# A closing norm whose last two feature tiles are squared one by one, and a feed-forward entry whose coarse products go first

## The reference, cut to what matters

```
def _rmsnorm(x, g):
    y = xf * lax.rsqrt(jnp.mean(xf * xf, axis=-1, keepdims=True) + EPS)
    return (y * g)
def _swiglu(x, w_up, w_down):
    g, u = jnp.split(x @ w_up, 2, axis=-1)
    return (jax.nn.silu(g) * u) @ w_down
for layer in range(DEPTH):
    x = x + 0.5 * _rmsnorm(_swiglu(_rmsnorm(x, ng[0]), w_ffn_up[layer, 0], w_ffn_down[layer, 0]), ng[1])
    h = _rmsnorm(x, ng[2])
    h = mixer(h)
    x = x + _rmsnorm(h, ng[3])
    x = x + 0.5 * _rmsnorm(_swiglu(_rmsnorm(x, ng[4]), w_ffn_up[layer, 1], w_ffn_down[layer, 1]), ng[5])
```

## Time and profile before

| | us |
|---|---|
| median of 3 runs | 2816.47 (2815.74 to 2819.28) |
| the profiled execution | 2812.93 |
| its span in the trace | 2811.2 |
| PE busy | 2674.3 (95%) |
| DVE busy | 1547.3 (55%) |
| ACT busy | 1154.2 (41%) |
| POOL busy | 273.4 (10%) |

### The profile page before, as it was taken

How to read it: one execution, slowest core, us unless ns; L and a number is a source line. 1 busy time by engine, 2 the same in 40 slices (tenths; PEclk the granted TensorE clock), 3 DMA queues, 4 the chain that set the end, 5 groups by cost and what they waited for, 6 DMA issues and landing times.

```text
span 2811.2 us, 51786 instructions
## 1 busy us (share of the span) xinstructions
PE 2674.3 (95%) x22016; PEld 2509.7 (89%) x22016; DVE 1547.3 (55%) x1978; ACT 1154.2 (41%) x1515; POOL 273.4 (10%) x294
## 2 busy tenths in 40 slices
PE   7998999899999899999999989999999989988998
PEld 7997887899999886699999978799999978877998
DVE  5546835655555445465465543465555558446554
ACT  4334444444433344343344333343343335435432
POOL 1000004100100225110010000010010000042000
PEclk9999999999999999999999999999999999998999
DMA  5544532454544535444455453455455444134543
GB/s 192 164 146 132 150 85 66 153 164 147 166 163 142 187 114 164 136 143 161 147 171 165 138 168 108 128 166 164 147 168 164 139 144 150 57 101 143 165 142 100
DMA packets 415626, 404.23 MB, mean 144 GB/s; under 512 B 14786, under 2 KB 411950, under 8 KB 415086
## 3 DMA queue, kind: packets, MB, share of 16 engines
q1 hardware_dynamic: 411348, 397.42, 44.9%
q0 software_dynamic: 4096, 4.20, 0.5%
HBM read 385.19 MB, written 16.39 MB: 143 GB/s over the span
## 4 chain that ended last, share of the span: by engine, by line
PE 88%; DVE 7%; ACT 2%; POOL 2%; issue 1%; DMA 0%; SPq 0%; DVEq 0%; POOLq 0%; ACTq 0%
PE psum L351 22%; PE psum L352 22%; PE psum L353 22%; POOL fbuf L406 1%; DVE x L537 1%; DVE y L535 1%; PE psum L2641 1%; PE psum L389 1%; PE psum L1115 1%; PE psum L1098 1%; PE psum L984 1%; DVE xn_lo L470 1%; PE psum L2040 1%; DVE w_lo L333 1%; PE psum L985 1%
## 5 line engine op out<-in xcount | busy, mean ns | idle before, releaser
L333 DVE TENSOR_TENSOR w_lo<-raw,w_hi 128x2048 fp32r<-128x2048 f32 (+3 forms) x366 | 753.4, 2058 | 555.5 <-ACT w_hi L326 555.4
L351 PE MATMUL psum<-xn_hi,w_hi 128*128 128x288 f32 x3296 | 987.2, 300 | 20.4 <-DVE xn_lo L1690 7.5
L352 PE MATMUL psum<-xn_lo,w_hi 128*128 128x288 f32 x3296 | 978.6, 297 | 0.0
L353 PE MATMUL psum<-xn_hi,w_lo 128*128 128x288 f32 x3296 | 975.2, 296 | 0.0
L326 ACT ACTIVATE w_hi<-raw 128x2048 fp32r<-128x2048 f32 (+3 forms) x366 | 623.9, 1705 | 785.2 <-PE psum L353 720.9
L351 PEld LDWEIGHTS psum<-xn_hi,w_hi 128*128 128x128 f32 x3296 | 623.9, 189 | 31.7 <-issue 16.4
L353 PEld LDWEIGHTS psum<-xn_hi,w_lo 128*128 128x128 f32 x3296 | 626.8, 190 | 0.0
L352 PEld LDWEIGHTS psum<-xn_lo,w_hi 128*128 128x128 f32 x3296 | 625.4, 190 | 0.4
L352 PE MATMUL psum<-h_lo,w_hi 128*128 128x288 f32 x1408 | 415.5, 295 | 0.0
L353 PE MATMUL psum<-h_hi,w_lo 128*128 128x288 f32 x1408 | 415.0, 295 | 0.0
L351 PE MATMUL psum<-h_hi,w_hi 128*128 128x288 f32 x1408 | 413.3, 294 | 0.0
(11 more groups left out here) (561 smaller groups left out, 3126.1 us busy)
## 6 DMA issues: line engine op xcount, KB each, us to landing
raw<-w_ffn_up SPq DMA_DIRECT2D x176, 1024.0 KB, 5.1
raw<-w_ffn_down SPq DMA_DIRECT2D x64, 768.0 KB, 4.4
raw<-w_ffn_down SPq DMA_DIRECT2D x64, 640.0 KB, 4.0
raw<-gdn_w_in SPq DMA_DIRECT2D x32, 1024.0 KB, 5.7
raw<-mlstm_w_in SPq DMA_DIRECT2D x12, 1024.0 KB, 5.4
raw<-gdn_w_out SPq DMA_DIRECT2D x8, 1024.0 KB, 6.8
raw<-cache_mla_latent SPq DMA_DIRECT2D x64, 128.0 KB, 2.2
a_split<-cache_mla_latent SPq DMA_DIRECT2D x64, 128.0 KB, 2.3
```

Source lines behind the costliest of these rows:

```text
L333: dve.tensor_tensor(wview(w_lo[slot(u, i)], u), wview(raw[u % NRAW], u), wview(w_hi[slot(u, i)], u).bitcast(F32), ALU.subtract).then_inc(l ...
L351: pe.matmul(out, wh[:, k, c], hi(k), start=st, stop=False)
L352: pe.matmul(out, wh[:, k, c], lo(k), start=False, stop=False)
L353: last = pe.matmul(out, wl[:, k, c], hi(k), start=False, stop=sp_)
```

## The change

Three edits. (1) In `act_square_y`, the last pair (i = 3) is squared tile by tile: tile 6 when PE has finished m = 0 of the last unit (a new semaphore `half_used`), tile 7 when the unit is done. Each raises `sq_ready`, so that a closing now counts five squares instead of four (`squares_before`). DVE takes tile 6 behind the first, tile 7 behind the second. (2) PE's product of `sq_total` moves from behind the last unit to between its m = 0 and its m = 1 (`pe_leave_part`); its waits move with it. The products of tiles 6 and 7 each wait for their own square. (3) In `pe_ffn` each tile k is done in two passes: first the 8 matmuls that need the coarse part of x alone (they wait for `xhi_ready`), then the 4 with its rest (they wait for `xlo_ready`).

```
-        def pe_unit(pe, u, outs, hi, lo, start, stop, i=0, ready=None, late=0):
+        def pe_unit(pe, u, outs, hi, lo, start, stop, i=0, ready=None, late=0, leave=None):
...
+                if leave is not None and m == 0:
+                    last.then_inc(half_used, 1)
+                    pe_leave_part(pe, leave)
...
+        half_used = sem("half_used")
+        squares_before = lambda q: H * q + q // 2
...
+        def pe_leave_part(pe, n):
+
+            pe.wait_ge(y_copied, H * n + 1)
+            pe.wait_ge(sq_sum, summed(2 * n + 1))
+            pe.matmul(psum[:, 1, 0:T], ones, sq_total, start=True, stop=False)
+
         def pe_leave_sums(pe, n):
 
-            q = 2 * n + 1
-            pe.wait_ge(y_copied, H * n + 1)
-            pe.wait_ge(sq_sum, summed(q))
-            pe.matmul(psum[:, 1, 0:T], ones, sq_total, start=True, stop=False)
-            pe.wait_ge(sq_ready, H * q + H)
             for k in range(2 * H - 2, 2 * H):
+                pe.wait_ge(sq_ready, squares_before(2 * n + 1) + k - H + 2)
                 last = pe.matmul(psum[:, 1, 0:T], ones, sq[:, k, :], start=False, stop=k == KC - 1)
...
-            dve.wait_ge(sq_ready, H * (2 * n + 1) + i + 1)
             for k in (2 * i, 2 * i + 1):
+                dve.wait_ge(sq_ready, squares_before(2 * n + 1) + i + 1 + (i == H - 1) * (k % 2))
                 last = dve.tensor_scalar(y[:, k, :], psum[:, k, 0:T], gain(l, g, k), None, ALU.mult)
...
+            if i == H - 1:
+                act.wait_ge(half_used, n + 1)
+                act.activation(sq[:, 2 * i, :], psum[:, 2 * i, 0:T], ACT.Square).then_inc(sq_ready, 1)
+                act.wait_ge(unit_used, u + 1)
+                act.activation(sq[:, 2 * i + 1, :], psum[:, 2 * i + 1, 0:T], ACT.Square).then_inc(sq_ready, 1)
+                return
...
             for k in range(KC):
-                pe.wait_ge(xlo_ready, entered(n) + k + 1)
+                pe.wait_ge(xhi_ready, entered(n) + k + 1)
                 for g, (hi, lo) in enumerate(first_two):
                     wh, wl = wview(hi, u0 + g), wview(lo, u0 + g)
                     for m in range(2):
                         out, c = psum[:, 4 + 2 * g + m, 0:T], slice(m * P, (m + 1) * P)
                         pe.matmul(out, wh[:, k, c], xn_hi[:, k, :], start=k == 0, stop=False)
-                        pe.matmul(out, wh[:, k, c], xn_lo[:, k, :], start=False, stop=False)
-                        last = pe.matmul(out, wl[:, k, c], xn_hi[:, k, :], start=False, stop=k == KC - 1)
+                        pe.matmul(out, wl[:, k, c], xn_hi[:, k, :], start=False, stop=False)
+                pe.wait_ge(xlo_ready, entered(n) + k + 1)
+                for g, (hi, lo) in enumerate(first_two):
+                    wh = wview(hi, u0 + g)
+                    for m in range(2):
+                        out, c = psum[:, 4 + 2 * g + m, 0:T], slice(m * P, (m + 1) * P)
+                        last = pe.matmul(out, wh[:, k, c], xn_lo[:, k, :], start=False, stop=k == KC - 1)
                     if k == KC - 1:
                         last.then_inc(unit_used, 1)
```

More of the change, by code:

```diff
@@ L382, in trunk @@
         entered = lambda n: sum(cuts(m) for m in range(n))
+        half_used = sem("half_used")
+        squares_before = lambda q: H * q + q // 2
         def pe_sum_squares(pe, q, i):
-            pe.wait_ge(sq_ready, H * q + i + 1)
+            pe.wait_ge(sq_ready, squares_before(q) + i + 1)
             for k in (2 * i, 2 * i + 1):
@@ L400, in pool_sums @@
             done, chunks = steps_before(q), range(2, H if q % 2 == 0 else H - 1)
-            pool.wait_ge(sq_ready, H * q + (2 if q % 2 else H))
+            pool.wait_ge(sq_ready, squares_before(q) + (2 if q % 2 else H))
             pool.tensor_tensor(sq_part, sq[:, 0:2, :], sq[:, 2:4, :], ALU.add).then_inc(sum_step, 1)
             for j, i in enumerate(chunks):
-                pool.wait_ge(sq_ready, H * q + i + 1)
+                pool.wait_ge(sq_ready, squares_before(q) + i + 1)
                 pool.wait_ge(sum_step, done + j + 1)
@@ L543, in pe_out @@
                 pe_unit(pe, u0 + i, [psum[:, 2 * i, 0:T], psum[:, 2 * i + 1, 0:T]], hi, lo, True, True,
-                        ready=ready if i == 0 else None)
+                        ready=ready if i == 0 else None, leave=n if i == H - 1 else None)
             pe_leave_sums(pe, n)
@@ L608, in pe_ffn @@
                     pe_unit(pe, u0 + 2 * PAIRS + DU * i + q, [psum[:, 2 * i, 0:T], psum[:, 2 * i + 1, 0:T]],
-                            lambda k: h_hi[:, k0 + k, :], lambda k: h_lo[:, k0 + k, :], q == 0, q == DU - 1)
+                            lambda k: h_hi[:, k0 + k, :], lambda k: h_lo[:, k0 + k, :], q == 0, q == DU - 1,
+                            leave=n if i == H - 1 and q == DU - 1 else None)
                     k0 += nk
```

## The result

The changed kernel takes 2831.09 us (median of 5, 2829.89 to 2833.60) against 2816.44 (median of 5, 2814.79 to 2819.28): ratio 1.0055, 95% interval 1.0044 to 1.0066. It is 14.65 us slower. The forecast was 2823.8 us, slower by 7.3, with a range up to 2831.0; the direction held, the size was half of what came, and the result lies 0.1 us beyond the range.

What follows compares the result with a forecast made beforehand. PE was taken to set the time except at boundaries between sublayers. Closings -2.4 us, low clock behind entries +8.5 and sums delayed by DVE +1.2 made +7.3, so 2823.8 us, range 2812 to 2831.

Steps and rivals of the forecast that it cites:

- The closing of a feed-forward: Closing behind the last unit: +0.49 us moved product, -0.24 shorter last square, -0.49 tile 6's product under cover; net -0.24.
- The entry: Feed-forward entry: PE starts 0.72 us earlier, but POOL's sum still releases the next work; no direct gain, longer second wait.
- The price of a low stretch: Behind the entry's wait for POOL, each stretch at granted clock 0.50 costs PE its whole 1.71 us.
- The displacement: Entry's end: DVE's split of the fourth unit gets in front of POOL's last step, making POOL's sum 2.3 us late.
- I take five of seven: Behind PE's wait for POOL at seven feed-forward entries, five get a stretch at granted clock 0.50: +8.5 us.
- an edge: PE waits: 2.37 us was followed by a low clock, 2.35 was not, so the limit was put near 2.4 us.
- I count half a case: Feed-forward entries: DVE getting ahead of POOL's last step, 2.3 us late each time, counted as half a case: +1.2 us.
- the closings together: All twelve closings, including PE's added wait in four mixers: -2.4 us, with ends at -4 and +0.5.
- a stand of 0.1 us for POOL's total: Mid unit in each of four mixers: PE waits 0.1 us for POOL's closing sum; +0.5 us in all.
- the forecast's own upper end: Top of the forecast's case: low clock behind all seven entries' waits and two sums delayed by DVE, 2830.7 us.
- the clock mostly holds: Rival: none to three of seven waits behind the entries bring a low clock; 2814.1 to 2819.2 us, chance 0.38.

Runs made afterwards that it cites:

- the closing edits alone: Kernel before plus split squares of tiles 6 and 7 and the moved `sq_total` product, feed-forward entry as before: 2815.30 us against 2815.43, ratio 0.9997.
- the entry edit alone: Kernel before plus only the feed-forward entry's coarse-part matmuls first, closings as before: 2824.93 us against 2815.43, ratio 1.0033.

## Why the prediction was right and wrong

Right, by its own steps:
- *The closing of a feed-forward.* -0.24 us each was forecast, and -0.24 to -0.25 is what the traces of the change and of the closing edits alone have. The root comes 1.59 us behind the last matmul's start; 1.58 was forecast.
- *The entry.* No direct gain, PE's first wait at 2.70 us, its second at 2.07 or longer: measured 2.71 and 2.01 to 2.19 at five entries. At the two without a low stretch 3.8 was forecast; the 5.5 measured are 3.5 and the displacement.
- *The price of a low stretch* behind the wait, 1.71 us: 1.5 to 1.6 at the five entries with a single one, 1.8 and 2.0 at the two with a longer one.
- *The displacement* of POOL's last step by DVE, with its cause. Holding DVE back took it away.

Wrong was the size. Two terms of the sum were too small:
- *"I take five of seven"* low stretches behind the second wait, 8.5 us. Seven of seven came, 11.4 us. I had set single waits of 2.35 and 2.37 us against each other as an edge. In the changed kernel's execution the same 2.35 us wait in a mixer (PE at L351, behind a split) was followed by a low stretch too, and so it was in 10 of the 13 profiled executions. Of the waits of 2.0 to 2.3 us for POOL at the entries 12 of 13 were, all but one of 2.00 us in the run with the entry edit alone. A single wait that had none was no edge: the same wait can go either way in the next execution. The trace of before also held a wait nearer to the forecast's 2.07 us than either (2.07, PE at L1115, 2476.57 us), with the clock kept at 1.00; it was not among the rows, and one such wait would have misled as the one of 2.35 did.
- *"I count half a case"* of displacement, 1.2 us. The profiled execution has two, 3.8 us. I had the mechanism but took too few entries without a low stretch, since I looked at the shorter first wait alone and not at the closing ahead of it: by the count above, 1 entry of 14 had none with the early start alone, and 14 of 28 with both edits. How the closing acts on the clock in the entry isn't shown; its last products now follow the unit without a gap. The price was 1.9 us, not 2.3.

A third term was too good: the closings together, -2.4 us, gave 1.9. In a mixer I forecast a stand of 0.1 us for POOL's total, and it is 0.20, with 0.08 more behind the product. (Four times 0.1 are 0.4, too, not the 0.5 of the sum.)

Seven low stretches and two displaced entries were the forecast's own upper end, 2830.7, and the result lies just beyond the range. That it came so near is partly luck, since nothing bounded the displaced entries at two; the range should have been wider. 13.3 of the 14.65 us are accounted for; the rest wasn't tracked down. It is less than what executions differ by: the four mixers, with the same program, took between 1017.0 and 1026.0 us in four of the profiled executions.

The rival "the clock mostly holds" (0.38) fell. The Trainium skill (TensorE: Matmul & The Clock Gate, "HAM oscillation — how this bites in real kernels") warns only of longer gaps. Taken as a promise that shorter ones are safe it doesn't fit this case: waits of 2.0 to 2.2 us were followed by a low clock at all five entries of the changed kernel that had one.

## What to carry to other kernels

An earlier start is worth nothing on an engine that waits at the end of the stage for another; and on PE the slack it makes isn't free, since the clock can fall behind it, where the work is no longer hidden. Ask of each edit that makes an engine ready sooner which of its waits grows, and which engine's next instruction is then set free to get in the way. The same edit turned from a loss of 9.5 us into a gain (5.0 us by the traces) once the chain that released PE had been cut: shorten the chain that ends last first, then start early. And a wait that is put into the middle of a stream of matmuls has to be checked at each kind of place: it was free in the feed-forwards and ate the whole gain in the mixers.

## What the runs showed of the hardware

- PE waits of 2.0 to 2.2 us for POOL were followed by a granted clock of 0.50 at all five entries of the changed kernel that had one, and at 12 of 13 in all profiled executions (2.0 to 2.3 us); of waits of up to 1.6 us for POOL at an entry none was. Work without use in the wait (2.1 us of it) kept the clock at 1.00, three times out of three.
- A low stretch inside the entry did good in the changed kernel: where it was missing, PE ended early, waited 5.5 us, and DVE's next instruction got in front of POOL's, and the entry took 18.4 us instead of 16.5. So a stage with slack ran worse when its PE was faster. With POOL's chain a step shorter it no longer did (15.0 us without a low stretch, 15.1 to 16.5 with one).
- POOL's step of 288 columns took 2.72 us instead of 0.80 behind a DVE instruction with two SBUF inputs that had started ahead of it, and 0.79 with that instruction held back.
